# Retention remainders shared by GpSimd and VectorE, and another order of work in block 0 of a hybrid decoder trunk

## What is computed

```python
h = _rmsnorm(x, norm_w)
z = jnp.einsum('btd,dc->btc', h, w_in)
gq, gk, gv, gg, glr, rq, rk, rv, rg = _split_cols(z)
la = jax.nn.log_sigmoid(glr @ gla_w2 + gla_b) / GLA_GATE_TAU          # gated linear attention (GLA)
q_b, k_b = _rope(rq, pos), _rope(rk, pos) * RET_DK ** -0.5            # retention
o_a, s_gla_new = _gla_chunked(q_a, k_a, v_a, la, s_gla)               # decode tokens: _gla_recurrent
o_b, s_ret_new = _ret_chunked(q_b, k_b, v_b, s_ret)                   # decode tokens: _ret_recurrent
o_a = rms_norm_per_head(o_a) * gla_norm_w * silu(gg)
o_b = (group_norm_per_head(o_b) * ret_norm_w + ret_norm_b) * silu(rg)
y = x + jnp.einsum('btc,cd->btd', concat(o_a, o_b), w_out)
```

## Time and profile before

| | |
|---|---|
| median of 3 runs | 1674.09 us (1673.62 to 1674.43) |
| profiled execution: time | 1673.73 us |
| profiled execution: span | 1671.9 us |
| TensorE busy | 1646.9 us, 99% |
| TensorE weight loads | 1349.1 us, 81% |
| VectorE busy | 1046.5 us, 63% |
| GpSimd busy | 854.1 us, 51% |
| ScalarE busy | 615.2 us, 37% |

### The profile page before, as it was taken

One profiled execution on the slowest core, in us unless ns is written; L12 is line 12 of the kernel. 1 busy time (PEld: TensorE's weight loads), 2 busy tenths in 40 slices (PEclk: granted clock), 3 DMA queues, 4 the chain that ended last, 5 costly groups with the idle time before them and its releaser, 6 DMA issues.

```text
span 1671.9 us, 26271 instructions
## 1 busy us (share of the span) xinstructions
PE 1646.9 (99%) x9770; PEld 1349.1 (81%) x9770; DVE 1046.5 (63%) x2372; ACT 615.2 (37%) x1159; POOL 854.1 (51%) x661
## 2 busy tenths in 40 slices
PE   6999999999999999999999999999999999999998
PEld 4888778888788887888878888788887888878886
DVE  7743576867765565547755466767887457784474
ACT  4413344233342343423443234342334324342342
POOL 4443645546454464454544445556554545554465
PEclk9999999999999999999999999999999999999999
DMA  7534657656564464366643656466864377453553
GB/s 265 166 105 100 177 201 224 181 162 176 181 186 129 103 198 138 114 155 160 190 133 96 155 140 187 164 176 182 194 184 139 114 163 161 161 170 105 142 156 138
DMA packets 384096, 266.33 MB, mean 159 GB/s; under 512 B 286560, under 2 KB 288992, under 8 KB 383968
## 3 DMA queue, kind: packets, MB, share of 16 engines
q1 hardware_dynamic: 310096, 130.14, 30.9%
q10 hardware_dynamic: 73872, 134.51, 24.6%
HBM read 217.51 MB, written 47.05 MB: 158 GB/s over the span
## 4 chain that ended last, share of the span: by engine, by line
PE 95%; POOL 2%; DVE 1%; DMA 1%; ACT 0%; issue 0%; ACTq 0%; POOLq 0%; SPq 0%
PE bank L718 82%; PE bank L977 3%; PE bank L983 2%; PE bank L781 1%; PE bank L961 1%; PE bank L939 1%; POOL w_lo L272 1%; PE bank L918 1%; PE bank L685 1%; POOL m_lo L652 1%; PE bank L922 1%; PE bank L739 1%; PE bank L994 0%; PE bank L791 0%; PE bank L897 0%; DMA w_stage<-in_w_slots 0%
## 5 line engine op out<-in xcount | busy, mean ns | idle before, releaser
L272 POOL TENSOR_TENSOR w_lo<-w_stage,w_hi 128x512 fp32r<-128x512 f32 x264 | 369.3, 1419 | 327.0 <-ACT w_hi L265 326.9
L718 PE MATMUL bank<-h_hi,w_hi 128*128 128x512 f32 x1024 | 408.5, 399 | 4.2 <-DVE h_lo L355 4.2
L718 PE MATMUL bank<-h_lo,w_hi 128*128 128x512 f32 x1024 | 399.8, 390 | 0.0
L718 PE MATMUL bank<-h_hi,w_lo 128*128 128x512 f32 x1024 | 399.4, 390 | 0.0
L272 POOL TENSOR_TENSOR w_lo<-ss,w_hi 128x512 fp32r<-128x512 f32 x164 | 223.0, 1380 | 206.4 <-ACT w_hi L265 206.2
L265 ACT ACTIVATE w_hi<-w_stage 128x512 fp32r<-128x512 f32 x264 | 152.9, 624 | 372.5 <-PE bank L718 326.2
L718 PEld LDWEIGHTS bank<-h_hi,w_hi 128*128 128x128 f32 x1024 | 192.5, 188 | 55.6 <-issue 8.1
L718 PEld LDWEIGHTS bank<-h_hi,w_lo 128*128 128x128 f32 x1024 | 192.6, 188 | 41.1
L718 PEld LDWEIGHTS bank<-h_lo,w_hi 128*128 128x128 f32 x1024 | 192.8, 188 | 37.2
L718 PE MATMUL bank<-w_hi,m_hi 128*128 128x512 f32 x512 | 201.7, 394 | 2.5 <-POOL m_lo L652 1.9
L718 PE MATMUL bank<-w_hi,h_hi 128*128 128x512 f32 x512 | 201.1, 393 | 0.0
(11 more groups left out here) (217 smaller groups left out, 2215.6 us busy)
## 6 DMA issues: line engine op xcount, KB each, us to landing
w_stage<-in_w_slots ACTq DMA_DIRECT2D x264, 256.0 KB, 3.5
ss<-in_w_slots ACTq DMA_DIRECT2D x164, 256.0 KB, 3.6
v_b<-in_w_slots ACTq DMA_DIRECT2D x84, 256.0 KB, 3.4
region<-in_x_prompt SPq DMA_DIRECT2D x32, 512.0 KB, 4.4
out_o_rows<-region SPq DMA_DIRECT2D x64, 256.0 KB, 3.5
region<-out_o_rows SPq DMA_DIRECT2D x192, 64.0 KB, 3.1
xn<-in_x_t SPq DMA_DIRECT2D x16, 512.0 KB, 4.9
out_k_rows<-region SPq DMA_DIRECT2D x32, 256.0 KB, 3.9
```

Of the source, the lines that this page charges most:

```text
L272: pool.tensor_tensor(w_lo[:, r, c], stage(h), w_hi[:, r, c].bitcast(f32), ALU.subtract).then_inc(lo_done, 1)
L718: i = pe.matmul(P[q][:, :], x, y, start=(s == 0 and kk == 0 and c == 0), stop=(s == 3 and kk == 1 and c == 2), skip_group_check=True)
```

## The change

In every block, GpSimd takes the remainders of the retention rows h = 0 and 1 (slots 23 and 24, one each) and VectorE those of h = 2 and 3 (slot 24, ahead of its work for the decode tokens there). A new semaphore `mlo_first` counts GpSimd's two; `mlo_sb` counts the six of VectorE. `mixed_rest` no longer waits for GpSimd's four.

In block 0:

- The gate rows (`hT_slot0`) and the decode tokens' gate come behind slot 2 instead of ahead of it; the gate's expansion goes into slot 3, and all that follows from it on ScalarE and VectorE is a slot later (`late`).
- At the start ScalarE rounds h k = 0 before the second weight half, and weight halves 2 and 3 behind k = 2 and 3; GpSimd takes their remainders ahead of the decode tokens' rsqrt; the loads of halves 4 and 5 are issued behind k = 1.
- The decode tokens' norm is one step of k sooner; `gmask` is made behind their start.
- `next_stats` moves from slot 2 to slot 8, GpSimd's rsqrt from slot 8 to slot 9.

In every block the queries are read out of their banks (`queries`) at slot 5 ahead of the second log gate, where that is in slot 5 too (block 0), and else where they were.

```diff
@@ SP
-                    sp.wait_ge(mlo_sb.sem, mlo_sb.at(n - 1, 8))
+                    sp.wait_ge(mlo_sb.sem, mlo_sb.at(n - 1, 6))
...
-                sp.wait_ge(mlo_sb.sem, mlo_sb.at(n, 2))
+                sp.wait_ge(mlo_first.sem, mlo_first.at(n, 2))
@@ GpSimd
             for h in range(2):
                 split_lo(pool, h)
+            for h in range(2, 2 * AHEAD):
+                split_lo(pool, h)
             pool.wait_ge(s_v.sem, s_v.at(0, V_NV - V_LAST))
             rsqrt(srs[:, :], svar[:, :], s_p.sem)
-            for h in range(2, 2 * AHEAD):
-                split_lo(pool, h)
...
-                        if w == 8 and n < NBLK - 1:
+                        if w == (9 if n == 0 else 8) and n < NBLK - 1:
                             pool.wait_ge(xstat.sem, xstat.at(n + 1, 4))
                             rsqrt(xrs[:, :], xvar[:, :], rstd_x.sem)
...
-                        for h in {23: (0, 1), 24: (2,), 25: (3,)}.get(w, ()):
+                        if w in (23, 24):
+                            h = w - 23
                             pool.wait_ge(mhi_sb.sem, mhi_sb.at(n, h + 1))
-                            pool.tensor_tensor(m_lo[:, 4 + h, :], ret_t[h], m_hi[:, 4 + h, :].bitcast(f32), ALU.subtract).then_inc(mlo_sb.sem, 1)
+                            pool.tensor_tensor(m_lo[:, 4 + h, :], ret_t[h], m_hi[:, 4 + h, :].bitcast(f32), ALU.subtract).then_inc(mlo_first.sem, 1)
@@ TensorE
-                        if kind == 0 and n > 0:
+                        if kind == 0:
                             sample_gate()
...
-                        if u == 6:
-                            pe.wait_ge(mlo_sb.sem, mlo_sb.at(n, 2 * s + 2))
+                        if u == 6 and s == 0:
+                            pe.wait_ge(mlo_first.sem, mlo_first.at(n, 2))
+                        elif u == 6:
+                            pe.wait_ge(mlo_sb.sem, mlo_sb.at(n, 2 * s))
...
-                            if n == 0 and u == 0 and s == 1:
-                                if q == 0:
-                                    sample_transposed(0)
-                                if q == 1:
-                                    gate_expand()
-                                if q == 2:
-                                    sample_gate()
+                            if n == 0 and w == 2 and q == 0:
+                                sample_transposed(0)
+                            if n == 0 and w == 3 and q == 0:
+                                gate_expand()
...
-                            if w == 2:
+                            if w == 2 + int(n == 0):
                                 pe.wait_ge(lrs_sb.sem, lrs_sb.at(l, 1))
...
-                            if w == 6:
+                            if w == 6 + int(n == 0):
+                                pe.wait_ge(s_v.sem, s_v.at(l, V_LA))
                                 z_transposed(X[:, 256:384], 0)
...
                             first_slot()
-                            hT_slot0()
                             continue
...
+                        if n == 0 and w == 2:
+                            hT_slot0()
@@ ScalarE
             split_hi(act, 0)
+            next_hi(act, 0, 0)
             split_hi(act, 1)
-            load_half(act, 4)
-            load_half(act, 5)
-            for k in range(KT):
+            for k in range(1, KT):
                 next_hi(act, 0, k)
-                if k in (3, 5):
-                    split_hi(act, (k + 1) // 2)
+                if k == 1:
+                    load_half(act, 4)
+                    load_half(act, 5)
+                if k in (2, 3):
+                    split_hi(act, k)
...
-                        if w == 2:
+                        if w == 2 + late:
                             for hf, src in ((0, ATT), (1, OB)):
                                 act.wait_ge(gate_x.sem, gate_x.at(n, hf + 1))
@@ VectorE
-                if k == 7:
+                if k == 6:
                     sample_norm(0)
...
-                            if w == 4:
+                            if w == 4 + late:
                                 sample_gate()
...
-                        vec.wait_ge(mlo_sb.sem, mlo_sb.at(n, 4))
                         vec.wait_ge(mhi_sb.sem, mhi_sb.at(n, 4 + h + 1))
...
+                    def mixed_rest_ret(h):
+
+                        vec.wait_ge(mhi_sb.sem, mhi_sb.at(n, h + 1))
+                        vec.tensor_tensor(m_lo[:, 4 + h, :], ret_t[h], m_hi[:, 4 + h, :].bitcast(f32), ALU.subtract).then_inc(mlo_sb.sem, 1)
...
-                        if w in (3, 4):
-                            hf = w - 3
+                        if w == 5:
+                            queries()
+                        if w in (3 + late, 4 + late):
+                            hf = w - 3 - late
...
-                        if w == (2 if n == 0 else 1) and n < NBLK - 1:
+                        if w == (8 if n == 0 else 1) and n < NBLK - 1:
                             next_stats(vec, n + 1)
...
+                        if w == 24:
+                            mixed_rest_ret(2)
+                            mixed_rest_ret(3)
```

More of the change, by code:

```diff
@@ L204, in build @@
         xstat, xn_sb, ystat, yn_sb = Count(sem("xstat"), 4, base=-4), Count(sem("xn_sb"), 1, base=-NBLK), Count(sem("ystat"), 4), Count(sem("yn_sb"), 4)
-        rstd_o, rstd_x, rstd_y, mlo_sb = Count(sem("rstd_o"), 8), Count(sem("rstd_x"), 1, base=-1), Count(sem("rstd_y"), 1), Count(sem("mlo_sb"), 8)
+        rstd_o, rstd_x, rstd_y, mlo_sb = Count(sem("rstd_o"), 8), Count(sem("rstd_x"), 1, base=-1), Count(sem("rstd_y"), 1), Count(sem("mlo_sb"), 6)
+        mlo_first = Count(sem("mlo_first"), 2)
         ya_sb, yw_sb, last_st, last_rs, last_sb, last_out = (sem(n) for n in ("ya_sb", "yw_sb", "last_st", "last_rs", "last_sb", "last_out"))
@@ L756, in unit_slot @@
                     def unit_slot(u, s):
+                        w = 4 * u + s + 1
                         first = n * HALVES + 2 * (4 * u + s)
                         pe.wait_ge(lo_done, first + 2)
-                        if u == 6:
-                            pe.wait_ge(mlo_sb.sem, mlo_sb.at(n, 2 * s + 2))
+                        if u == 6 and s == 0:
+                            pe.wait_ge(mlo_first.sem, mlo_first.at(n, 2))
+                        elif u == 6:
+                            pe.wait_ge(mlo_sb.sem, mlo_sb.at(n, 2 * s))
                         if n == 0 and u == 0:
@@ L777, in unit_slot @@
                             if s == 1:
+                                if u == 0:
+                                    pe.wait_ge(s_v.sem, s_v.at(l, V_H))
                                 free_sample_bank(u)
@@ L1080, in sample_work @@
                             return
-                        if w == 2:
+                        if w == 2 + late:
                             act.wait_ge(lrs_ps.sem, lrs_ps.at(l, 1))
                             nc.scalar.activation(lr_s[0:RANK, :], X[0:RANK, 128:136], ACT.Copy).then_inc(lrs_sb.sem, 1)
-                        if w == 3:
+                        if w == 3 + late:
                             act.wait_ge(gx_ps.sem, gx_ps.at(l, 1))
@@ L1090, in sample_work @@
                             nc.scalar.activation(gt[:, :], gt[:, :], ACT.Ln, bias=1.0).then_inc(gl_s.sem, 1)
-                        if w in (7, 14, 22, 26):
-                            c = (7, 14, 22, 26).index(w)
+                        if w in (7 + late, 14, 22, 26):
+                            c = (7 + late, 14, 22, 26).index(w)
                             col = (0, 8, 4, 12)[c]
@@ L1104, in sample_work @@
                                                      ACT.Tanh, scale=0.5).then_inc(tg_s.sem, 1)
+                    late = int(n == 0)
                     for w in range(SLOTS):
-                        if w == (1 if n > 0 else 2):
-                            act.wait_ge(slot_used, n * SLOTS + (1 if n > 0 else 2) + RING)
+                        if w == (1 if n > 0 else 3):
+                            act.wait_ge(slot_used, n * SLOTS + w + RING)
                             act.wait_ge(const_in, 96)
@@ L1593, in mixed_rest, with queries @@
                     def mixed_rest(h):
-                        vec.wait_ge(mlo_sb.sem, mlo_sb.at(n, 4))
                         vec.wait_ge(mhi_sb.sem, mhi_sb.at(n, 4 + h + 1))
                         vec.tensor_tensor(m_lo[:, h, :], o_t[:, h, :], m_hi[:, h, :].bitcast(f32), ALU.subtract).then_inc(mlo_sb.sem, 1)
-                    def rotate():
+                    def mixed_rest_ret(h):
+                        vec.wait_ge(mhi_sb.sem, mhi_sb.at(n, h + 1))
+                        vec.tensor_tensor(m_lo[:, 4 + h, :], ret_t[h], m_hi[:, 4 + h, :].bitcast(f32), ALU.subtract).then_inc(mlo_sb.sem, 1)
+                    def queries():
                         for p in range(2):
@@ L1608, in rotate @@
                             vec.tensor_tensor(q4[0], q4[1], qdec[:, p, :].unsqueeze(1).to_broadcast([128, TPB, TOK]), ALU.mult).then_inc(q_raw.sem, 1)
```

(4 more changed lines are left out.)

2 lines of the change are left out of this document (removed).

## The result

The kernel after takes 1679.42 us, median of 7 runs (1678.3 to 1682.03), against 1674.09 (1673.58 to 1674.89, 7 runs): ratio 1.0035, 95% interval 1.0026 to 1.0044. It is slower: the interval lies above 1. Its profiled execution took 1680.81 us with a span of 1679.0 and TensorE busy 1650.0. What follows accounts for the 7.1 us between these two executions, not for the 5.3 us between the medians.

What follows compares the result with a forecast made beforehand. TensorE's row of matmuls was taken as the bound. 1673.73 - 3.5 (slot 26) + 3.4 (blocks 1 and 5) + 3.7 (slot 9) = 1677.3 us, 1677.7 as median; it said 1677.6, range 1672.0 to 1681.5.

Steps and rivals of the forecast that it cites:

- waits that trade places: Main forecast: waits removed at slot 26 reappear at slot 9 and in blocks 1 and 5; 1677.6 us, chance 0.50.
- Slot 26: Slot 26 across blocks: TensorE's waits for GpSimd's m_lo go, 3.5 us gained, bounds 1.9 and 3.6.
- Blocks 1 and 5: Slot 25: VectorE's two m_lo delay silu(1), costing 2.5 us in block 1 and 0.9 in block 5, +3.4 together.
- No wait came from there: Slot 25: GpSimd's second m_lo takes the former third's place, where blocks 2 to 7 showed no wait.
- Slot 9: Block 0: next_stats at slot 8 delays the first scores; TensorE resumes at about 82.5, +3.7 us, bounds 2.4 and 5.1.
- w_lo of slot 10 is queued behind it ... that costs nothing: Block 0: w_lo queued behind GpSimd's moved rsqrt is wanted by TensorE only two slots later, so no cost.
- The head: Start of block 0: reordering puts TensorE 0 to 2.2 us ahead after slot 3; not added to the sum.
- The clock: Rival, chance 0.14: TensorE's clock falls in the slot 9 wait of about 4 us, some 1.7 us lost; 1679.3 us.
- Early keys: Rival, chance 0.12: block 0's rotation starts 3.6 us sooner, keys land near 67, slot 9 costs nothing; 1669.9 us.

Runs made afterwards that it cites:

- experiment 6: Kernel before with only the remainders' split, VectorE's two at slot 25 behind silu(1) instead of slot 24: 1671.34 us, ratio 0.9984.
- experiment 11: Kernel of experiment 6 with GpSimd's two remainders both at slot 23 instead of one each at slots 23 and 24: 1671.5 us, ratio 0.9985.
- experiment 8: Kernel after with the remainders as before the change and next_stats of block 0 at slot 7, to test the head alone: 1674.21 us, ratio 0.9998.
- experiment 3: Kernel after with 40 idle matmuls on TensorE between slot 9 and the masked scores of block 0: 1678.01 us, ratio 1.0031.
- experiment 4: Kernel before with only next_stats at slot 8 and GpSimd's rsqrt at slot 9 of block 0: 1683.38 us, ratio 1.0054.
- experiment 7: Kernel after with next_stats of block 0 at slot 7 and VectorE's two remainders at slot 25: 1670.96 us, ratio 0.9984.
- experiment 2: Kernel after with VectorE's two remainders of slot 24 moved behind the decode tokens' affine and gate: 1680.6 us, ratio 1.0041.
- experiment 1: Kernel after with next_stats of block 0 at slot 7 instead of slot 8, GpSimd's rsqrt staying at slot 9: 1672.94 us, ratio 0.9991.

## Why the prediction came out as it did

The forecast's mechanism, waits that trade places, is what happened, and the time (1679.4, said 1677.6, range 1672.0 to 1681.5) is 1.8 us above the value. That it came so near is in part luck. Between the profiled executions the sum said +3.6 us and the rows show +7.1: slot 9 and the falling clock cost 5.2 us more than the sum had, blocks 1 and 5 and slot 26 about 1.7 less, and the profiled execution is 1.4 above its median. By the steps of the sum:

- **Slot 26, said -3.5.** Right in kind, a little too small. The five blocks without any other difference gained 2.8, and block 0 gained 0.8 between slot 10 (+8.86) and its end (+8.08): 3.6 for six of the seven waits. The seventh lay in block 5, and with the 0.45 that was said for it the gain is about 4.0.
- **Blocks 1 and 5, said +3.4.** Right in kind and too large. Block 1 came to +1.5 (its wait grew from 0.59 to 2.09), where 2.5 was said. Block 5 came to +0.3 net of its wait at slot 26, so to about 0.8, where 0.9 was said. Together that is 2.2 or 2.3. I had charged two full turns of 1.25 us. The two m_lo and the decode tokens' products together took fewer. VectorE, block 1, kernel after:

```profile
398.33 3.29 DVE L1608 TENSOR_TENSOR m_lo<-tmp,m_hi 128x512 fp32r<-128x512 f32 x2 [6.24 <-ACT m_hi L1205]
...
402.07 1.97 DVE L1398 SCALAR_TENSOR_TENSOR sg_s<-sg_s,z_t 128x32 f32<-128x32 f32 x2
404.08 0.29 DVE L1403 TENSOR_TENSOR ms<-o_s,sg_s 128x32 f32<-128x32 f32 x2
404.29 2.47 DVE L1581 SCALAR_TENSOR_TENSOR region<-region,bank 128x512 f32<-128x512 f32 x4
```

  The m_lo took 3.29, but the decode tokens' products behind them took 2.3 us instead of 4.7 (390.06 to 394.79 in the kernel before).
- **"No wait came from there" (slot 25, GpSimd's second m_lo).** True in the kernel after, where g_t hides it. As soon as g_t is in time it is the next wait, 1.05 us (experiments 6 and 11).
- **Slot 9, said +3.7, TensorE resuming at 82.5.** This is the step that was mis-sized most: TensorE resumed at 85.63, +6.8. Two parts of it failed. I took the rotation to start 0.3 us earlier; it started 1.7 later, four of its eight operations on the keys took 1.67 us where only one did before, and the second half of the keys was stored at 59.48 instead of 54.95. Since that store landed in 2.6 us instead of 5.7, the keys came only 1.3 later. And the decode rotation was to give back up to 2.0 us, while "w_lo of slot 10 is queued behind it ... that costs nothing": this w_lo held VectorE's three copies, so that the rotation took 3.5 us (81.3 to 84.8), as long as before (74.4 to 77.8). The move cost TensorE nothing as a late w_lo; it cost VectorE its turn.
- **The head, said 0 to 2.2 us ahead.** Wrong for this execution, 1.0 behind, and nothing in the medians (experiment 8). The first product came 1.34 us sooner (up to 1.2 was said), but the matmuls stayed 0.43 us apart some 5 us longer than before. The term for the head left that out. It is no loss beside the +6.8 but the 1.0 in it: the wait behind slot 9 ends with VectorE, whenever TensorE comes to it.
- **The clock, a rival at 0.14, +1.7.** It happened, +2.05 (experiment 3 takes it away). The Trainium skill (TensorE: Matmul & The Clock Gate, What's actually happening) has the array fall back after an idle stretch; the windows agree, 1.00, then 0.51. I gave this rival too little, though I had forecast a wait of about 4 us myself.
- **Early keys, 0.12.** It didn't come about, neither in the kernel after (keys at 73.15) nor with the statistics moved alone (experiment 4). It left out SyncE, which stores the keys behind a load that waits for TensorE's slot 6.

Added up, each block net: 1.0 (head) + 5.8 (wait) + 2.05 (clock) - 3.6 (slot 26) + 1.5 + 0.3 = 7.05, against 7.08 between the profiled executions.

What stays open: why the store of the keys' second half lands in 2.4 to 2.6 us where it is issued 4 us behind the load of x_t (kernel after, experiment 3), and in 5.7 to 6.9 where it is issued within 1.0 us of it (kernel before, experiments 4 and 6); and what sets the moment in the head at which the matmuls come closer. In kernels with the new head that was between 21 and 25 us, in those with the old one between 19 and 22, and I found no edit that moves it but the idle matmuls. What the head is worth by itself is open with it. Experiment 6 or 7 would be the version to keep; which of them is better can't be told.

## What to carry to other kernels

Before moving independent work next to an engine's wait, look on which side of the waiting instruction it lands: with the same eight statistics behind the wait for the keys the kernel took 6.5 us longer than with them ahead of it. Price a wait of several microseconds on TensorE with the slow matmuls that follow it. Where two engines hold each other up, look at what is queued on the other one too: GpSimd's w_lo behind the moved rsqrt made 2.6 us out of 0.5 for three small copies of VectorE. And follow a transfer to the engine that issues it: SyncE's loop, not the rotation, set when the keys were stored in experiment 4.

## What the hardware showed unexpectedly

- The low clock outlasts the wait that brought it on. After a wait of 5.65 us the rows run slow to about 89.9 (2.05 us lost), after one of 7.39 us to about 91.7 (experiment 4). Forty matmuls that do nothing keep it up. It needn't fall in the wait: in experiment 2 the wait was 5.06 us, the granted clock was 1.00 throughout it, fell at 85.3, just behind its end (85.19), and was back at 88.7; slot 10 opened 4.79 us behind 85.19, 1.7 lost.
- GpSimd doesn't always hold VectorE. During its rsqrt of 128x4 (81.41 to 82.43) four VectorE operations of 128x16 took 0.23 us each:

```profile
81.49 0.23 DVE L1301 TENSOR_SCALAR z_t<-z_t,small 128x16 f32<-128x16 f32 x1
```

  The same line took 1.03 us in experiment 1 and 1.02 in the kernel before. And silu(1), whose inputs are `region` and a PSUM bank, took 2.49 us for four (0.62 each) while GpSimd did its m_lo from 394.38 to 395.66 (experiment 6): it wasn't held.
